# Spreading a head's exponent row with a 128-row matmul in place of a 64-row one, in a hybrid attention and SSD layer

## What is computed

```python
# forgetting attention, per head: c is the running sum of log-sigmoid forget gates over the tokens
s = einsum('bhqd,bhkd->bhqk', q, k) * scale
s = s + c[..., :, None] - c[..., None, :]
pr = softmax(where(k_pos <= q_pos, s, -inf));  y_A = pr @ v

# SSD, per head: a_cum is the running sum of dt * A
seg   = a_cum[:, :, :, None, :] - a_cum[:, :, None, :, :]
decay = exp(where(causal, seg, -inf))
y_diag = (C B^T * decay) @ (dt * x)
```

## Time and profile before

| | |
|---|---|
| time, median of 3 runs | 1260.08 us (1260.0 to 1260.17) |
| time of the profiled execution | 1260.43 us |
| its span, first to last instruction | 1258.7 us |
| TensorE (PE) busy | 1245.7 us, 99% of the span |
| VectorE (DVE) busy | 856.7 us, 68% |
| ScalarE (ACT) busy | 616.9 us, 49% |
| GpSimd (POOL) busy | 60.8 us, 5% |
| mean granted TensorE clock | 0.998 of 2.4 GHz |
| DMA | 226.94 MB, 180 GB/s mean |

### The profile page before, as it was taken

The page is one execution under the profiler, slowest core; times in us unless marked ns, Lnnn a source line. Parts: engine busy times, 40 slices in busy tenths (PEclk is TensorE's granted clock), DMA queues, the critical chain, the costliest instruction groups (busy, mean ns, idle before and its releaser), DMA issues.

```text
span 1258.7 us, 21432 instructions
## 1 busy us (share of the span) xinstructions
PE 1245.7 (99%) x7838; PEld 1108.7 (88%) x7838; DVE 856.7 (68%) x1120; ACT 616.9 (49%) x810; POOL 60.8 (5%) x66
## 2 busy tenths in 40 slices
PE   8999999999999999999999999999999999999997
PEld 7999998789999888888888888888888888888885
DVE  6698777677678776767767677676746464646554
ACT  6544555656444454444444454454444344444555
POOL 2000000001213100000000000000001010101000
PEclk9999999999999999999999999999999999999999
DMA  8566555344656666666666666666665656566652
GB/s 256 168 183 184 157 146 155 114 114 125 199 172 203 186 193 186 185 196 183 191 193 185 194 187 187 194 187 188 191 190 166 216 160 217 164 212 202 198 185 101
DMA packets 165885, 226.94 MB, mean 180 GB/s; under 512 B 10209, under 2 KB 101381, under 8 KB 165701
## 3 DMA queue, kind: packets, MB, share of 16 engines
q1 hardware_dynamic: 165732, 225.90, 59.3%
q0 software_dynamic: 96, 0.26, 0.1%
HBM read 224.03 MB, written 2.10 MB: 180 GB/s over the span
## 4 chain that ended last, share of the span: by engine, by line
PE 97%; DVE 1%; DMA 1%; ACT 0%; SPq 0%; issue 0%; ACTq 0%; DVEq 0%
PE ps L344 39%; PE ps L346 19%; PE ps L332 8%; PE ps L333 8%; PE ps L334 8%; PE ps L372 4%; PE ps L374 4%; PE ps L373 3%; DMA w_raw<-in_w_in 1%; PE ps L764 1%; PE ps L767 1%; PE ps L808 1%; DVE h_parts L1243 0%; PE ps L791 0%; PE ps L821 0%; PE ps L778 0%
## 5 line engine op out<-in xcount | busy, mean ns | idle before, releaser
L317 DVE TENSOR_TENSOR w_lo<-w_raw,w_hi 128x1024 fp32r<-128x1024 f32 x413 | 505.9, 1230 | 318.2 <-ACT w_hi L312 317.5
L312 ACT ACTIVATE w_hi<-w_raw 128x1024 fp32r<-128x1024 f32 x413 | 435.9, 1059 | 459.4 <-PE ps L346 341.2
L344 PE MATMUL ps<-h_parts,w_hi 128*128 128x512 f32 x1408 | 488.6, 394 | 0.0
L346 PE MATMUL ps<-h_parts,w_lo 128*128 128x256 f32 x1408 | 390.2, 277 | 0.0
L344 PEld LDWEIGHTS ps<-h_parts,w_hi 128*128 128x128 f32 x1408 | 264.0, 188 | 61.5
L346 PEld LDWEIGHTS ps<-h_parts,w_lo 128*128 128x128 f32 x1408 | 264.2, 188 | 0.0
L344 PE MATMUL ps<-act_parts,w_hi 128*128 (+1 forms) x704 | 244.4, 392 | 0.0
L346 PE MATMUL ps<-act_parts,w_lo 128*128 (+1 forms) x704 | 196.8, 280 | 0.0
L332 PE MATMUL ps<-h_parts,w_hi 128*128 128x256 f32 x576 | 165.8, 288 | 0.6 <-DVE w_lo L317 0.6
L333 PE MATMUL ps<-h_parts,w_hi 128*128 128x256 f32 x576 | 162.9, 283 | 0.0
L334 PE MATMUL ps<-h_parts,w_lo 128*128 128x256 f32 x576 | 162.9, 283 | 0.0
(11 more groups left out here) (248 smaller groups left out, 1115.3 us busy)
## 6 DMA issues: line engine op xcount, KB each, us to landing
w_raw<-in_w_gate_up SPq DMA_DIRECT2D x352, 256.0 KB, 3.2
w_raw<-in_w_in SPq DMA_DIRECT2D x88, 512.0 KB, 3.7
w_raw<-in_w_down SPq DMA_DIRECT2D x88, 512.0 KB, 4.6
w_raw<-in_w_out SPq DMA_DIRECT2D x32, 512.0 KB, 4.6
w_raw<-in_w_ple_gate SPq DMA_DIRECT2D x32, 512.0 KB, 4.6
w_raw<-in_w_ple_proj SPq DMA_DIRECT2D x4, 512.0 KB, 5.3
out_x<-out_tok SPq DMA_DIRECT2D x8, 256.0 KB, 2.9
xtok<-in_x SPq DMA_DIRECT2D x3, 512.0 KB, 9.1
```

The costliest lines, as they stand in the source:

```text
L312: act.activation(parts(n)[0], w_raw[:, n % RING, :], ACT.Copy).then_inc(w_hi_made, 1)
L317: dve.tensor_tensor(lo, w_raw[:, n % RING, :], hi, ALU.subtract).then_inc(w_lo_made, 1)
L344: pe.matmul(ps[:, bank_of[m], :], hi, both.rearrange("p b t -> p (b t)"), start=first and k == 0, stop=False, skip_group_check=True)
L346: mm = pe.matmul(ps[:, bank_of[m], T:2 * T], lo, both[:, 0, :], start=False, stop=last and k == 1, skip_group_check=True)
```

## The change

The moving operand gets 128 rows, the stationary one too. Rows 64 to 127 of `ssd_row` and `fox_row` are filled with zeros, copied from the zeroed half of `kE`. The products of the added rows are zero.

```diff
-        ssd_row, fox_row = at("ssd_row", [4 * H, 3 * P], F32R), at("fox_row", [4 * H, 3 * P], F32R)
+        ssd_row, fox_row = at("ssd_row", [P, 3 * P], F32R), at("fox_row", [P, 3 * P], F32R)
...
-                both = 4 * H
-                pe.matmul(ps[:, bank, 0:3 * P], sel[0:both, j:j + 1].to_broadcast([both, P]), row[:, :],
+                pe.matmul(ps[:, bank, 0:3 * P], sel[:, j:j + 1].to_broadcast([P, P]), row[:, :],
                           start=start, stop=False, skip_group_check=True)
...
                     dve.tensor_copy(sel[:, :], sel_f[:, :])
+                link(dve.tensor_copy(dst[2 * n:P, :], kE[2 * n:P, 0:2, :].rearrange("p a t -> p (a t)")[:, 0:3 * P]))
                 link(dve.tensor_copy(dst[0:n, :], src))
                 dve.tensor_tensor(dst[n:2 * n, :], src, dst[0:n, :], ALU.subtract).then_inc(cum_ready, 1)
```

## The result

| | before | after |
|---|---|---|
| median of 5 executions | 1260.0 us (1259.88 to 1260.17) | 1252.23 us (1251.71 to 1254.93) |
| profiled execution, its span | 1260.43, 1258.7 us | 1251.71, 1250.0 us |
| ratio | | 0.9943, 95% interval 0.9933 to 0.9954 |

The kernel became 7.8 us faster by the medians. Two of the five executions after lie at 1254.8 and 1254.9, the other three at 1251.7 to 1252.2; experiments 2, 7 and 8 are about these two. First the change itself, in the profile of the kernel after. Its line 763 is line 764 of before, 766 is 767, 807 is 808, 820 is 821, 1395 is 1396. The kernels of the experiments shift these numbers by one to three lines; the tile names tell which instruction is meant.

What follows compares the result with a forecast made beforehand. TensorE, busy 99% of the span, was taken as the bound. 16 x 0.245 (SSD) plus 16 x 0.295 (attention) plus 0.1 gave 8.7 us saved: 1260.1 to 1251.4 us, range 1249.9 to 1254.8.

Steps and rivals of the forecast that it cites:

- The SSD head: Line 821's last matmul to line 767: 0.52 us becomes 0.285, saving 0.235 in each of 16 heads.
- The attention head: Line 808's second pass to line 767: 0.68 us becomes 0.395, saving 0.285 in each of 16 heads.
- The term that was mis-sized: Before line 767, the mask matmul: its exposed weight load would become hidden, saving 0.01 us per head.
- The term put at nothing: Operand supply to TensorE in both head stages: would keep up with periods shortened to 3.6 and 4.5 us; nothing charged.
- The cause: Around line 764: switching between 128 and 64 rows drains TensorE, two drains per head, gaps of 0.09 us each.
- The change to bfloat16: Rival for the gap behind line 764: the data type causes it, so 5.5 us saved, 1254.6 us; chance 8%.
- The load in the open: Rival at line 764: its load stays exposed behind the matmul in flight; 6.0 us saved, 1254.1 us; chance 4%.
- No effect: Rival: gaps hang on something both kernels share; nothing saved, 1260.1 us, or 1260.8 with the copies; chance 7%.
- slow streaming: Rival at line 764: 128 rows stream at plain float32 pace, 0.66 us instead of 0.175; 1267.0 us; chance 3%.
- The copies: Two 64 x 384 VectorE copies near 85 and 88 us: 0.76 us in all, hidden by some 3 us of lead.
- Signs that were named wrongly: Profile after: no idle before loads of lines 764 and 767; line 764's record about 0.335 us in attention.
- the first rival: Bfloat16 causes the gap behind line 764; sign: line 767's load keeps 0.19 us idle before it; 1254.6 us; chance 8%.

Runs made afterwards that it cites:

- experiment 2: Against the changed kernel: zero copies still made, but the row matmul multiplies 64 rows again; median 1260.22 us, ratio 1.0002, one execution at 1263.09.
- experiment 7: Against the changed kernel with one 256-column mask matmul per head: fourth piece of x loaded ahead of the third weight chunk; 1250.43 us, ratio 0.9922.
- experiment 8: Against the changed kernel, its two mask matmuls kept: fourth piece of x loaded ahead of the third weight chunk; 1251.77 us, ratio 0.9936.
- experiment 1: The changed kernel timed again with no edit; median 1251.74 us, ratio 0.9941 to the kernel before.
- Experiment 5: Against the changed kernel: 96 rows in place of 128 in the row matmul; 1252.15 us, ratio 0.9936.
- experiment 6: Against the kernel before: the 64-row matmul of 384 columns cut into two 64-row matmuls of 192 columns; 1260.87 us, ratio 1.0008.
- experiment 3: Against the changed kernel: 128 rows in the SSD heads' row matmul alone, 64 in the attention heads; 1256.56 us, ratio 0.9971.

## Why the prediction was right, point by point

**The bound.** TensorE bounded the kernel, and what it saved arrived at the end: some 8.15 us in the trace, and 1259.95 - 1251.74 = 8.2 us between the medians of experiment 1, whose batch holds one late execution of five. Predicted were 8.7. The range of 1249.9 to 1254.8 holds the median of 1252.23, with some luck: two of its five executions were late for a reason that the prediction didn't know, and with a third the median would have been 1254.8, at the upper edge.

**The SSD head.** Predicted 0.285 us from the last output matmul to the mask, measured 0.29. **The attention head.** Predicted 0.395 from the second score pass, so 0.615 from the first; measured 0.61.

**The term that was mis-sized.** "Line 767's own load ... I put it at 0.01" was an error of reading: nothing was saved there. The mask's load starts with its matmul as before, and from the mask to the chunk's second matmul it is 0.30 us in SSD and 0.41 in attention in both kernels. Without this term the sum is 14 x 0.235 + 2 x 0.285 + 16 x 0.285 = 8.4 us.

**The term put at nothing.** The prediction charged nothing for the supply, since TensorE didn't wait in the kernel before, and that was nearly right. It named waits for a head's probabilities as a sign that something is given back, and the loads show it: 0.4 us once for `probT_lo` and 0.2 us once for `prob`, of which some 0.2 us reach the end. With it the sum is 8.2 us, as measured.

**The cause.** The two gaps went when the rows changed and nothing else. Experiment 5 shows that 96 rows serve as well, experiment 6 that two 64-row matmuls in a row pay once, and experiment 3 that each stage pays for itself. The Trainium skill's rule ("TensorEngine Tiling (Array Packing)", Key Properties), that a change of tiling mode drains TensorE, and not a change of tile within it, agrees with all three runs: 0.09 us on the way into 64 rows and 0.09 on the way out. That TensorE drains in these gaps is the Trainium skill's reading; the runs show the gaps. A change in the columns of the stationary operand has none: line 820 has 64 columns there, and the row matmul with 128 follows at its full pace, its load starting with line 820's last matmul (153.52).

**The rivals.** The change to bfloat16: line 766 still follows an fp32r matmul, and the 0.09 us behind that one are gone, by the stretches of 0.29 and 0.61. The load in the open: it starts at 236.23, with the score pass ahead of it, although both have 128 rows. The Trainium skill's rule for that rival ("TensorE: Matmul & The Clock Gate", Part 3), that a load overlaps with matmuls in flight only when their row groups differ, isn't what this trace does. No effect, and slow streaming: both excluded by the same slots.

**The copies.** Predicted 0.34 us each and 0.38 with their wait, 0.76 in all. The records are 0.36, but VectorE's work behind both came later by more: w_lo runs at 89.94, and in the kernel before at 89.51, which less the 0.57 of the earlier start is 88.94. So 1.0 us for both, since the casts ahead of line 1397 (that of `sel` at 85.66, and that of `ident_bf` before `fox_row`) used to overlap with it by 0.09 us, and now each stands clear. The cover of some 3 us was enough: experiment 2 has the copies and the time of the kernel before, and TensorE waits for nothing between 80 and 100 us.

**Signs that were named wrongly.** The prediction said that the mask's loads would lose their idle, and that the first rival would hold if they kept it. They kept it in attention (3.2 us), and the rival is false all the same: the load starts only when its own matmul does (236.62 both), but that matmul starts 0.39 us after the second score pass, which is just 0.22 and 0.175 and leaves no room for a gap. It also said that the row matmul's record would fall to 0.335 us in attention. It rose to 0.52: its record begins at 236.26, 0.03 us after the second pass began, long before that pass's 0.22 us of columns are through. Both were signs taken from single records. The profile models the ends of matmuls, so a record's length isn't a measurement of their work. The distances over the whole stretch, which the sum was built on, held to 0.01 us.

**What the median hid.** Not foreseen was that an execution can have a late piece of x and then half the clock for 3.4 us, as the profiled one of experiment 2 had. If the two late executions of the result are such, it is this that widens the interval. Whether the change makes this more frequent is open. The kernel before showed it in none of 46 executions, the changed kernel in three of ten; if the two had the same rate, all three would fall among these ten with a chance of 0.4%. But the copies alone showed it in one of eleven and the 64-row pairs in one of ten (1263.69), and none of these kernels has a changed instruction before 80 us. No run here tells what in the changed programs would favour it.

## What to carry to other kernels

When a small matmul uses 64 rows or 32 between ones of 128, look at the start-to-start distances around it: here the switch to 64 rows cost two gaps of 0.09 us and an exposed load of up to 0.11 each time, and zero rows removed them for the price of two small copies in the whole program. Order the matmuls so that a load of 128 columns stands behind one with 256 moving columns and not behind one with 128. Measure a stretch from the start of the last undisturbed instruction to the start of the next, for a record's own length and the idle before a load can mislead by more than the whole effect.

## What the runs showed of the hardware that was not expected

- 96 rows behave as 128 do: idle before the loads 0.4 and 0.0 us in both, 1252.15 against 1251.74 us.
- The record of a matmul behind a second float32 pass begins 0.03 us after that pass does (236.23 to 236.26), where its columns can't be in work yet; the record is 0.19 us longer than the slot would make it (0.52 against 0.335).
- A wait of 2.2 us for one piece of the input at 13 to 16 us was followed by 3.4 us at half the granted clock (0.51) and cost this execution some 3 us: 1263.09 against 1260.22.
